# Scores of two half iterations in one place, and ScalarE's softplus half an iteration later, in a two-layer decoder step

## What is computed

```
z = einsum('bqhd,bkhd->bhqk', q, k) * scale + bias
log_1mb = where(mask, log_sigmoid(-z), 0)
tail = cumsum(log_1mb, reverse=True) - log_1mb
w = where(mask, exp(log_sigmoid(z) + tail), 0)
out = einsum('bhqk,bkhd->bqhd', w, v)
```

## Time and profile before

| | |
|---|---|
| median of 3 runs | 1409.45 us (1408.23 to 1413.83) |
| the profiled execution | 1408.98 us |
| its span, first to last instruction | 1407.3 us |
| TensorE busy | 1391.1 us, 99% |
| VectorE busy | 899.6 us, 64% |
| ScalarE busy | 734.5 us, 52% |
| GpSimd busy | 182.6 us, 13% |
| TensorE's granted clock, mean | 0.998 |
| HBM read and written | 242.10 MB and 5.53 MB, 176 GB/s over the span |

### The profile page before, as it was taken

The page is one execution under the profiler, slowest core; times in us unless marked ns, Lnnn a source line. Parts: engine busy times, 40 slices in busy tenths (PEclk is TensorE's granted clock), DMA queues, the critical chain, the costliest instruction groups (busy, mean ns, idle before and its releaser), DMA issues.

```text
span 1407.3 us, 26950 instructions
## 1 busy us (share of the span) xinstructions
PE 1391.1 (99%) x10551; PEld 1321.4 (94%) x10551; DVE 899.6 (64%) x1508; ACT 734.5 (52%) x1210; POOL 182.6 (13%) x333
## 2 busy tenths in 40 slices
PE   7999999999999999999999999999999999999998
PEld 6999999988878999999999999999888799999998
DVE  5666544669995876663367665346899858756542
ACT  4544434489766554443365444346887665444441
POOL 1020000323262110000000000021433510000000
PEclk9999999999999999999999999999999999999999
DMA  9575455577799595545545555564868895555541
GB/s 247 150 210 150 141 147 153 156 203 230 210 310 265 145 255 150 150 139 152 155 127 149 151 149 144 152 175 141 252 206 242 287 255 154 151 149 149 148 139 50
DMA packets 391554, 249.41 MB, mean 177 GB/s; under 512 B 16513, under 2 KB 379638, under 8 KB 391428
## 3 DMA queue, kind: packets, MB, share of 16 engines
q1 hardware_dynamic: 375602, 204.94, 51.2%
q0 software_dynamic: 15520, 42.62, 9.7%
q10 hardware_dynamic: 306, 0.13, 0.0%
HBM read 242.10 MB, written 5.53 MB: 176 GB/s over the span
## 4 chain that ended last, share of the span: by engine, by line
PE 94%; DVE 2%; ACT 1%; DMA 1%; issue 1%; SPq 0%; POOLq 0%; POOL 0%; DVEq 0%; ACTq 0%
PE bank L596 25%; PE bank L598 24%; PE bank L597 24%; PE bank L862 3%; PE bank L973 2%; PE bank L877 2%; PE bank L632 2%; PE bank L636 2%; PE bank L633 2%; PE bank L1050 1%; DMA raw<-in_ffn_w_gate 1%; PE bank L827 1%; PE bank L954 1%; PE bank L1168 1%; PE bank L1090 1%
## 5 line engine op out<-in xcount | busy, mean ns | idle before, releaser
L1602 DVE TENSOR_TENSOR w_l<-raw,w_h 128x1024 fp32r<-128x1024 f32 (+1 forms) x332 | 395.4, 1196 | 295.4 <-ACT w_h L1224 295.1
L596 PE MATMUL bank<-hh,w_h 128*128 128x320 f32 x1632 | 512.9, 314 | 0.0
L598 PE MATMUL bank<-hh,w_l 128*128 128x320 f32 x1632 | 504.4, 309 | 0.0
L597 PE MATMUL bank<-hl,w_h 128*128 128x320 f32 x1632 | 504.3, 309 | 0.0
L1224 ACT ACTIVATE w_h<-raw 128x1024 fp32r<-128x1024 f32 (+1 forms) x332 | 332.3, 1030 | 141.4 <-DMA raw<-in_ffn_w_down 101.4
L596 PEld LDWEIGHTS bank<-hh,w_h 128*128 128x128 f32 x1632 | 306.4, 188 | 11.8 <-issue 8.6
L597 PEld LDWEIGHTS bank<-hl,w_h 128*128 128x128 f32 x1632 | 306.5, 188 | 0.6
L598 PEld LDWEIGHTS bank<-hh,w_l 128*128 128x128 f32 x1632 | 306.4, 188 | 0.0
L596 PE MATMUL bank<-guh,w_h 128*128 128x320 f32 x704 | 217.7, 309 | 0.0
L598 PE MATMUL bank<-guh,w_l 128*128 128x320 f32 x704 | 217.4, 309 | 0.0
L597 PE MATMUL bank<-gul,w_h 128*128 128x320 f32 x704 | 217.4, 309 | 0.0
(11 more groups left out here) (297 smaller groups left out, 1604.9 us busy)
## 6 DMA issues: line engine op xcount, KB each, us to landing
raw<-in_ffn_w_gate SPq DMA_DIRECT2D x88, 512.0 KB, 4.0
raw<-in_ffn_w_up SPq DMA_DIRECT2D x88, 512.0 KB, 3.9
raw<-in_ffn_w_down SPq DMA_DIRECT2D x64, 448.0 KB, 3.8
raw<-in_w_in SPq DMA_DIRECT2D x44, 512.0 KB, 4.0
raw<-in_ffn_w_down SPq DMA_DIRECT2D x32, 512.0 KB, 4.0
kpg<-in_cache_sb_k SPq DMA_DIRECT2D x112, 128.0 KB, 3.3
kpg<-in_cache_sb_k POOLq DMA_DIRECT2D x112, 128.0 KB, 2.7
raw<-in_w_out SPq DMA_DIRECT2D x16, 512.0 KB, 6.9
```

Of the source, the lines that this page charges most:

```text
L596: pe.matmul(out, w_h[:, slot, k, :], rhs_h[:, k0 + k, :], start=first, stop=False)
L597: pe.matmul(out, w_h[:, slot, k, :], rhs_l[:, k0 + k, :], start=False, stop=False)
L598: last = pe.matmul(out, w_l[:, slot, k, :], rhs_h[:, k0 + k, :], start=False, stop=end)
L1602: V(dve.tensor_tensor(w_l[:, slot, 0:n, :], raw[:, slot, 0:n, :], w_h[:, slot, 0:n, :].bitcast(F32), ALU.subtract), sm["w_lo"])
```

## The change

It moves calls and adds no instruction. On TensorE the scores of h - 2 and h - 1 are made together, in the unit of an even h. On ScalarE both copies of turned keys go ahead of `place_scores`, `softplus` of an iteration goes into the unit of the next, odd h, between its two copies of keys (that of the last iteration stays in unit 21), and what stood at the end of unit 10 becomes `new_weights_and_gates` in unit 11. VectorE's, SyncE's and GpSimd's programs are as before.

```diff
@@ TensorE @@
                     if h < 2 * ITS:
                         turn_keys(h, (0, 1))
-                    if 0 < h <= 2 * ITS:
+                    if h and h % 2 == 0:
+                        scores(h - 2)
                         scores(h - 1)
...
                         turn_keys(last_h, (0, 1))
                         unit(u, out, hh, hl, part=range(5, 6))
-                        scores(h)
+                        if last_h % 2 == 0:
+                            scores(last_h - 2)
+                            scores(last_h - 1)
                         unit(u, out, hh, hl, part=range(6, 7))
@@ ScalarE @@
+                def new_weights_and_gates():
+
+                    act.wait_ge(*at("zn_lw", 1))
+                    A(nsa(zn[:, :, :], zn[:, :, :], ACT.Exp), sm["wn_ready"])
+                    act.wait_ge(*at("loga_neg", 1))
+                    A(nsa(dd[:, 1], dd[:, 1], ACT.Exp))
+                    A.settle()
+                    A(nsa(dd[:, 1], dd[:, 1], ACT.Ln, bias=1.0), sm["loga_l"])
+
...
                             copy_keys(h, (0, 1))
                         if m == 7:
                             place_queries()
-                        if h >= 2 and h % 2 == 0:
-                            place_scores(h // 2 - 1)
+                        if 3 <= h < 2 * ITS and h % 2:
+                            softplus((h - 1) // 2 - 1)
+                        if m == 11 and h == TURNS[m][0]:
+                            new_weights_and_gates()
                         if h == TURNS[m][0]:
                             hi(U + U_IN + m + 2)
                         if h < 2 * ITS:
...
                         if h >= 2 and h % 2 == 0:
-                            softplus(h // 2 - 1)
+                            place_scores(h // 2 - 1)
+                        if h == 2 * ITS:
+                            softplus(ITS - 1)
...
-                    if m == 10:
-                        act.wait_ge(*at("zn_lw", 1))
-                        A(nsa(zn[:, :, :], zn[:, :, :], ACT.Exp), sm["wn_ready"])
-                        act.wait_ge(*at("loga_neg", 1))
-                        A(nsa(dd[:, 1], dd[:, 1], ACT.Exp))
-                        A.settle()
-                        A(nsa(dd[:, 1], dd[:, 1], ACT.Ln, bias=1.0), sm["loga_l"])
```

## The result

The changed kernel takes **1428.88 us** (median of four runs, 1428.07 to 1431.27) against 1409.25 of the kernel before beside it (1408.23 to 1413.83): ratio 1.0146, 95% interval 1.0134 to 1.0158. It is 1.5% slower; forecast were 1425 us in a range of 1413 to 1433. The profiled execution is the slowest of the four, 1431.27 us with a span of 1429.6.

A forecast was written before the change was run, and what follows sets the result against it. TensorE was taken as the bound, with VectorE almost full in the stage. Late softplus costs 7.7 us a layer, pairs' gain included, 15.4 us on 1409.45: 1425 us, 1.1% slower, range 1413 to 1433.

The forecast's parts named there:

- main case: Units 9 to 22: VectorE waits in order for late softplus and delays TensorE; 15.4 us for two layers, 1425 us, chance 0.75.
- softplus at the turn plus 3.1 us: Units 14 to 20: softplus reaches VectorE 3.1 us after TensorE's turn starts: 0.78 to first copy, copies 0.95, softplus 1.20, signal 0.15.
- The path: Layer 0, unit 9 to khat in unit 22: step-by-step new start times, khat at 401.3 against 393.89, plus 7.4 us.
- TensorE's waits: TensorE would idle about 3 and 2 us for att in units 14 and 16, about 3 us at the khat turn.
- The 0.57 us before: At 342.36 in the old kernel, TensorE was said to stand 0.57 us for VectorE's copy into att.
- What was costed at nothing: Gates moved to unit 11, later value pages and w_out loads, and later key copies were all taken as hidden.
- the prediction's bound: Without cover from products and hi(), TensorE's turn of batches 2 and 3 would be late by up to 0.6 us.
- The pairs, minus 5.3 us: Two scores back to back take 1.86 us, saving 0.33 us a pair; eight pairs in two layers give minus 5.3 us.
- hidden case: Rival: softplus's wait is hidden and only the pairs count; 1404 us, chance 0.07.
- partly hidden one: Rival: TensorE waits only in units 14 and 16, the khat turn has more room; plus 8.6 us, 1418 us, chance 0.10.
- Value pages as a new wait: Rival: iteration 1's value pages, asked for later, hold TensorE up to 5.5 us a layer; 1436 us, chance 0.05.
- The clock: Rival: after the longest pauses of units 14 and 22 TensorE runs at 1.2 GHz, 3.6 us each, four times; 1439 us, chance 0.03.

The follow-up runs named there:

- experiment 1: Changed kernel with softplus put back at the end of the even unit, behind placing scores; 1416.22 us, ratio 1.0055 to the kernel before.
- (4): Changed kernel with softplus moved still further back, behind hi(), the high part of the weights; 1446.41 us, ratio 1.0264 to the kernel before.
- (7): Changed kernel with VectorE's log_weights also moved to the odd unit: with pairs 1412.92 us (1.0032), then with single scores 1408.87 us (1.0007).
- experiment 3: Changed kernel with single scores in each unit again, ScalarE's new order kept; 1426.19 us, ratio 1.0118 to the kernel before.
- experiments 4 and 6: 4: changed kernel, softplus behind hi(), 1446.41 us; 6: that kernel with 26, 18 and 9 unread products in units 14, 16 and 22, 1439.65 us.
- Experiment 2: Kernel before with only TensorE's part of the change, two scores together, ScalarE as it was; 1412.24 us, ratio 1.0028.
- first kernel of experiment 7: Changed kernel with VectorE's log_weights moved to the odd unit beside softplus, pairs of scores kept; 1412.92 us, ratio 1.0032 to the kernel before.
- experiment 8: Experiment 7's single-score kernel with pairs only in units 15, 17, 19: 1408.18 us (0.9999); six taps left out per layer: 1409.05 us single, 1408.53 us with pairs.

## Why the prediction was right, and where its terms were off

The number was in its range, and the mechanism of its main case is the one that the runs show: undoing softplus's place takes most of the loss (experiment 1), more of the dose gives more (4), moving the reader along takes all of ScalarE's part away (7), and without the pairs most of the loss is still there (3). Of the 4 us between the number and the median a part is the clock, which the main case left out. Step by step:

- **softplus at the turn plus 3.1 us.** log_weights started 3.23, 3.36, 3.37 and 3.71 us after the turns of units 14, 16, 18 and 20. The term was 0.1 to 0.6 too small each time. From the first copy of the keys on it took 2.43 to 2.45 us, where 2.30 were given. The rest is the copy's start: 0.78 us after the turn in unit 14, as forecast, but 0.93, 0.94 and 1.28 in the others, as ScalarE was still at other work. The steps of units 14, 16 and 20 reach TensorE and make 1.0 of the 1.4 us by which khat was missed.
- **The path.** Taking off the 0.20 us by which L783 came later in the profiled run: turn of unit 14 forecast 332.4, measured 332.84; level_prompt(1) 340.0 and 340.63; turn of 16, 352.1 and 352.79; level_prompt(3) 358.5 and 359.41; unit 18, 370.6 and 371.56; unit 20, 385.7 and 386.67; khat 401.3 and 402.74. It was 0.4 behind before the first of the four steps (log_weights(1) came at 310.47, not 310.0, and level_prompt(0) 1.2 us late, not 0.8), and 1.4 at the end. The layer cost 8.85, not 7.4 up to khat and 7.7 in all.
- **TensorE's waits.** About 3, 2 and 3 us were forecast for att, att and khat; the loads show 3.07, 2.04 and 2.08, and 1.52 before the turn of weights in unit 21 (none in the kernel before), which the prediction did not have: together 3.60 ahead of khat, for 3.1. VectorE's first three waits, forecast 1.8, 1.9 and 2.3, were 1.90, 2.17 and 2.42. At log_weights(6) it was to be 8.1 us behind and was 9.6 (390.58 - 380.76, less the 0.20). The 0.57 us before, which the prediction gives to VectorE's copy, are 0.41 of change of shape and 0.16 of waiting; its own sum takes only the 0.16 off.
- **What was costed at nothing.** The gates moved to unit 11 were hidden. The value pages were asked for at 394.84 (forecast 394) and waited for by nobody in this kernel; the timeline of SyncE's queue, kernel after, answers to the earlier trace rows:

```profile
394.84 4.35 SPq L436 DMA_DIRECT2D vpg0b<-in_cache_sb_v  x8
```

  ScalarE did wait 4.54 us for w_out, as shown above; the stretch from khat on is no longer for it. Keys came late twice a layer, by up to 0.6 us: the prediction's bound, which it took to be hidden.
- **The pairs, minus 5.3 us.** This step failed. The pair itself takes 1.86 us to the digit (303.04 to 304.90), but "the turn alone needs about 0.92" holds only where no product of another shape follows, and late keys took the rest. The pairs alone gave nothing in the stretch. In the changed kernel they cost about 1.6 us a layer (experiment 3). The sum of the main case was right on this all the same, as it does not use the minus 5.3: on its path the pair enters as 0.86 longer, twice, and 0.33 shorter, once.
- **The rivals.** The hidden case is excluded by TensorE's waits for att and khat, the partly hidden one by those ahead of khat. Value pages as a new wait did not occur here, and were 0.8 us at the most in kernels that don't have the main delay. The clock was real in part: it fell behind the pauses in layer 1 and not in layer 0, and cost about 1.5 us each where 3.6 were given. The prediction's reading that the kernel before has a lower clock "only in the last 7 us" is wrong (0.66 at 1110 us, below). The chance of 0.03 was for it as the whole course; as a part of the main case it should have stood there with 1 or 2 us for each pause. The Trainium skill's warning of idle gaps between bursts ("TensorE: Matmul & The Clock Gate", section "Why this matters for your kernels") agrees with experiments 4 and 6; that pauses of 3.07, 2.04 and 2.08 us passed without a cost in layer 0 shows that here it is a risk and not a certainty.

The account of the profiled execution: 1408.98 + 2 x 8.85 = 1426.7; two low-clock periods in layer 1's stretch 3.1; from khat to L636 in layer 1, where the third one lies, 1.3 more than before (81.74 against 80.42): 1431.1, measured 1431.27. The forecast for this execution was 1424.4. So of the 6.9 us missed 2.3 are the queue (8.85 a layer, not 7.7) and 4.4 the clock.

**Open.** Experiment 2 and the first kernel of experiment 7 (all pairs kept, main delay absent) are 0.3% slower than before though their stretches are not longer. Part of it lies between khat and L636. In a layer without a low clock there they need 79.2 and 79.3 us, with small waits for value pages (0.5 and 0.8 us in all), against 78.3 to 78.7 in the kernel before, with single scores and with the three pairs of experiment 8. That makes some 1.5 us for two layers. In experiment 8 the last two scores are single, so the value pages are asked for as early as before, and the loss is gone; but the early pairs are gone too, so the pages are not isolated as the cause. The other part goes with the clock: its mean over the runs is 0.9972 in both slow kernels and 0.9985 in both others, which at 1.4 us for 0.001 is some 1.8 us (an estimate). Why it is lower has not been seen, as the profiled run of the kernel with log_weights later was, at 1409.83 us, 3 below its own median.

## What to carry to other kernels

When one engine's step is moved later, look for every reader of its result in the other engines' in-order programs, and for what stands in the queue behind that reader: here two instructions of ScalarE, moved by half an iteration, cost 1.2% with single scores, mostly through VectorE's copies into att, which have nothing to do with them. In a stage where two engines are full, the delay is passed on almost whole, about the wait itself at each step, and the cure is to move the reader too. Work that is taken out of a unit in which its engine waits anyway saves nothing there, and costs its whole length in a unit that stands on the path. A saved switch of shape counts only if the instruction that follows doesn't bring its own.

## What was not expected of the hardware

- TensorE's clock falls behind pauses of 2 to 4.5 us, but not always: not in layer 0 of the changed kernel, but behind the waits for att in its layer 1 in both profiled runs, behind a pause of 2.39 in both layers with single scores, and in both layers of the kernel whose pauses are 4.51 and 3.12. A fall costs about 1.5 us in the changed kernel. Unread products in the pause keep it at 1.00 in all these windows, and with pauses that large the kernel becomes faster by 6.8 us for doing more.
- The clock also falls where TensorE does not pause. The windows of the kernel before, TensorE, in the value products of layer 1:

```profile
1105.00:1110.00 5.00, 5.00 (x71) 1.00 1.07 349
1110.00:1115.00 5.00, 5.00 (x41) 0.66 1.08 354
```

  TensorE is busy for all of both, and the DMA share is the same, yet the clock goes from 1.00 to 0.66. What sets this off wasn't tried. A single run's time goes with its mean clock wherever that differs by more than 0.001 between the runs (experiment 3: 0.998 at 1423.66 us, 0.992 at 1432.15).
- Some changes of the products' shape bring a pause in the weight loads: 0.17 us before 128x32 or 64x64 behind 128x128, and 0.41 behind a group of 128x32. From 64x64 back to 128x128 there is none of that size (0.07 us, 334.05 to 334.12 in the kernel before).
